# Forgetting attention rebuilt in a 16-head, 1024-token fp32 decoder step: split q and v stored by the projections, minima instead of maxima, GpSimd normalisation, halves copied by VectorE and added by DMA

## What is computed

```python
# layer 0: y = W_out(B * conv3(C * h)), then SwiGLU; layer 1: attention, then SwiGLU
k, v = split(x @ kv_w); logf = log_sigmoid(x @ f_w + f_b); cum = cumsum(logf)
q = x @ q_w
s = (q . k) * 64**-0.5 + cum[t] - cum[s]        # s <= t, else -inf
p = softmax(s); o = p @ v; y = o @ o_w
x = layer_norm(ALPHA * x + y)                    # after every mixer and every FFN
x = layer_norm(ALPHA * x + (silu(x @ g) * (x @ u)) @ w_down)
# outputs: y, k, v, logf, conv state, for the prompt and for the samples
```

## Time and profile before

| | |
|---|---|
| median of 3 runs | 2944.03 us (2940.56 to 2947.19) |
| span of the profiled execution | 2939.8 us |
| TensorE busy, mean granted clock | 2726.8 us, 0.951 |
| VectorE, ScalarE, GpSimd busy | 1279.7, 838.0, 822.3 us |
| k, v, q stage, us 1228 to 1545 | 317 us |
| between that stage and attention's first scores | 29 us |
| attention, us 1574 to 1981 | 407 us |

### The profile page before, as it was taken

The page is one execution under the profiler, slowest core; times in us unless marked ns, Lnnn a source line. Parts: engine busy times, 40 slices in busy tenths (PEclk is TensorE's granted clock), DMA queues, the critical chain, the costliest instruction groups (busy, mean ns, idle before and its releaser), DMA issues.

```text
span 2939.8 us, 44825 instructions
## 1 busy us (share of the span) xinstructions
PE 2726.8 (93%) x16971; PEld 2622.2 (89%) x16971; DVE 1279.7 (44%) x2212; ACT 838.0 (29%) x1463; POOL 822.3 (28%) x475
## 2 busy tenths in 40 slices
PE   8999959999999999699996889989799999999994
PEld 8999949999999999499994777779699999999994
DVE  3333582422222222850555888874733222222237
ACT  2111142111111111432224666652511111111114
POOL 2222252112212112532333333323612221212114
PEclk9999979999999999899997888889799999999996
DMA  4111101111111111022874454442011111111101
GB/s 131 43 50 43 45 22 44 44 44 44 46 56 44 51 44 44 15 74 77 262 245 129 125 133 124 123 126 65 22 44 44 44 57 45 51 44 44 51 15 58
DMA packets 214332, 206.47 MB, mean 70 GB/s; under 512 B 29239, under 2 KB 184887, under 8 KB 214188
## 3 DMA queue, kind: packets, MB, share of 16 engines
q1 hardware_dynamic: 209388, 187.25, 21.8%
q0 software_dynamic: 4800, 17.08, 1.7%
HBM read 178.76 MB, written 25.57 MB: 70 GB/s over the span
## 4 chain that ended last, share of the span: by engine, by line
PE 80%; DVE 10%; issue 5%; DMA 2%; ACT 1%; POOL 1%; SPq 0%; DVEq 0%; POOLq 0%; ACTq 0%
PE ps L1600 25%; PE ps L1601 24%; PE ps L1602 24%; DVE ss L1482 2%; PE ps L1859 2%; DVE ln_t L1271 1%; DVE ln_t L1275 1%; PE ps L1888 1%; DVE ln_d L1216 1%; DVE ptl L1507 1%; DMA k_prompt<-ktok 1%; PE ps L1874 1%; PE ps L1841 1%; PE ps L1837 1%; PE ps L1875 1%
## 5 line engine op out<-in xcount | busy, mean ns | idle before, releaser
L1600 PE MATMUL ps<-xh,whi 128*128 128x344 f32 x3288 | 1067.7, 325 | 28.2 <-POOL xl L663 18.0
L1601 PE MATMUL ps<-xl,whi 128*128 128x344 f32 x3288 | 1054.7, 321 | 0.0
L1602 PE MATMUL ps<-xh,wlo 128*128 128x344 f32 x3288 | 1054.5, 321 | 0.0
L617 POOL TENSOR_TENSOR wlo<-wraw,whi 128x1024 fp32r<-128x1024 f32 x197 | 481.3, 2448 | 1700.4 <-ACT whi L794 1700.4
L1600 PEld LDWEIGHTS ps<-xh,whi 128*128 128x128 f32 x3288 | 620.2, 189 | 56.8 <-POOL xl L663 34.3
L1602 PEld LDWEIGHTS ps<-xh,wlo 128*128 128x128 f32 x3288 | 621.8, 189 | 0.0
L1601 PEld LDWEIGHTS ps<-xl,whi 128*128 128x128 f32 x3288 | 621.6, 189 | 0.0
L1600 PE MATMUL ps<-zh,whi 128*128 128x344 f32 x1440 | 465.4, 323 | 17.4 <-DVE x L1343 9.4
L1601 PE MATMUL ps<-zl,whi 128*128 128x344 f32 x1440 | 463.7, 322 | 0.0
L1602 PE MATMUL ps<-zh,wlo 128*128 128x344 f32 x1440 | 461.7, 321 | 0.0
L1320 DVE TENSOR_TENSOR silu<-silu,ps 128x344 f32<-128x344 f32 x132 | 67.8, 513 | 875.6 <-PE ps L1602 875.6
(11 more groups left out here) (206 smaller groups left out, 2650.0 us busy)
## 6 DMA issues: line engine op xcount, KB each, us to landing
wraw<-ffn_w_gu SPq DMA_DIRECT2D x88, 512.0 KB, 3.8
wraw<-ffn_w_down SPq DMA_DIRECT2D x44, 512.0 KB, 3.5
kp<-cache_k SPq DMA_DIRECT2D x32, 512.0 KB, 5.4
vp<-cache_v SPq DMA_DIRECT2D x32, 512.0 KB, 3.5
wraw<-a_w_in SPq DMA_DIRECT2D x24, 512.0 KB, 3.8
wraw<-kv_w SPq DMA_DIRECT2D x16, 512.0 KB, 5.3
qd<-q_t SPq DMA_DIRECT2D x32, 256.0 KB, 4.7
kd<-k_t SPq DMA_DIRECT2D x32, 256.0 KB, 5.3
```

The lines of the kernel that those rows point to most:

```text
L617: pool.tensor_tensor(wlo[:, s, :], wraw[:, s, :], f32(whi[:, s, :]), ALU.subtract).then_inc(w_lo, 1)
L1600: pe.matmul(out, w_h, m_h, start=start, stop=False)
L1601: pe.matmul(out, w_h, m_l, start=False, stop=False)
L1602: return pe.matmul(out, w_l, m_h, start=False, stop=stop)
```

## The change

It rebuilds attention and what feeds it.

1. `q_t` in HBM gets two planes. `take_q` on ScalarE writes the high part, scaled with -QSCALE, and `q_low` on VectorE the low part, both out of PSUM; only `q_low` frees the bank. v goes the same way into a new `v_t` (`v_tokens`, `v_low`). In attention `qa` and `vhl` are loaded ready split; `qk_high`, `v_high`, attention's `q_low` and `v_low` go.
2. The scores are negated, the mask is +1e30, the bias row is `ccum`, VectorE takes the minimum, and ScalarE's exponential has scale -1. The negation L1488 goes.
3. Scores, mask, transposes and values leave out the blocks above the diagonal (`span`, `turned`).
4. All of `norm` runs on GpSimd as a tensor_scalar. GpSimd also does both halves of k's split (`k_split`).
5. VectorE copies all 128 rows of `values` to `oe` (`o_take`). SP stores the upper half to `o_t`, and GpSimd's queue adds the lower half there with an accumulating DMA (`add_halves`). The last pair is added in SBUF as before.
6. `wraw` and `wlo` share memory. A load of a weight block therefore waits until the unit that used the slot is over (`used`), instead of for the split of the block before.
7. `o_t` is read through five buffers, and the first unit of `o` takes k-block 7 of all chunks last (`first_o`).

```diff
+        whi = wa.put("whi", [P, WR, WCOLS], F32R)
+        wlo = wa.put("wlo", [P, WR, WCOLS], F32R)
+        wraw = Area(W_AT + WR * WCOLS * 4).put("wraw", [P, WR, WCOLS], F32)
...
+            def used(unit):
+                return full[NCH - 1], unit - WR + 1
...
             def load_kvq(it, keys):
+                first = isinstance(it, int) and it == 0
+                ends = ffn[0].at("down", FG * KB * NCH)
+                load(n0 + 3 * it, n0, w_kv[:, :, bass.ds(it * P + D, P)], ends if first else used(g0 + 3 * it))
...
+                    load(n0 + 3 * it + 1 + j, n0 + 1 + j, src, ends if first and j == 0 else used(g0 + 3 * it + 1 + j))
...
             for m in range(WR):
-                load(SLOTS["o"] + m, SLOTS["o"] + m, w_o[:, :, m * P:(m + 1) * P])
+                load(SLOTS["o"] + m, SLOTS["o"] + m, w_o[:, :, m * P:(m + 1) * P], used(UNITS["o"] + m))
             load_samples(KB - 1)
...
+            with sp.Fori(0, KB - 1) as b:
+                next_qk(b, 0)
+                load_v_page(b, 2)
+                load_v_page(b, 3)
+                next_qk(b, 1)
+                next_v(b, 0)
                 store_head(b, 0)
+                load_v_page(b + 1, 0)
+                load_v_page(b + 1, 1)
+                next_v(b, 1)
                 store_head(b, 1)
...
+            def k_split(b, e):
...
+                pool.wait_ge(qk_in[e], loaded)
+                pool.tensor_copy(kh[e][:, :], kd[e][:, :]).then_inc(at["khi"], 1)
                 pool.wait_ge(at["khi"], 2 * b + e + 1)
                 pool.tensor_tensor(kl[e][:, :], kd[e][:, :], f32(kh[e][:, :]), ALU.subtract).then_inc(at["klo"], 1)
...
+                for t in range(2):
+                    pool.tensor_scalar(ss[j][:, t, 0:span(st, t)], ss[j][:, t, 0:span(st, t)], ri[:, j, t:t + 1], None,
+                                       ALU.mult).then_inc(at["pnorm"], 1)
...
+                pool.dma_start(o_t[bass.ds(b, 1), e * DH:(e + 1) * DH, :].rearrange("a p t -> (a p) t"),
+                               oe[e][DH:P, :], accum_op=ALU.add).then_inc(oe_add[e], 16)
...
             with pool.Fori(0, KB - 1) as b:
+                norm(b, STEPS)
+                k_split(b + 1, 0)
+                for st in range(STEPS + 1, PAIR):
+                    norm(b, st)
+                add_halves(b, 0)
+                norm(b, PAIR)
+                k_split(b + 1, 1)
+                for st in range(PAIR + 1, PAIR + STEPS):
+                    norm(b, st)
+                add_halves(b, 1)
...
+                    act.activation(hl[:, 0, c * CH:c * CH + w], ps[:, c, 0:w], ACT.Copy, scale=-QSCALE).then_inc(kv["qh"], 1)
...
+            with dve.Fori(0, KB // 2) as it:
+                q_low(it, 0)
+                v_low(it)
+                q_low(it, 1)
...
             with dve.Fori(0, NS // 2) as it:
+                v_low(it + KB // 2)
                 for j in range(2):
...
-                    dve.wait_ge(at["sdr"], 2 * s + 2)
-                    dve.tensor_scalar(nm[:, j, :], mx[:, j, :], -1.0, None, ALU.mult).then_inc(at["neg"], 1)
...
+                dve.tensor_copy(oe[e][:, j * 2 * P:(j + 1) * 2 * P], ps[:, 6 + st % 2, 0:2 * P]).then_inc(at["odone"], 1)
...
+                    pe.wait_ge(at["pnorm"], 2 * s + 2)
...
+                blocks = [(2 * g, 0), (2 * g, 1)] + [(2 * g + 1, t) for t in range(2) if t or g < j]
...
+def span(st, t):
+    return P * (2 * (st % STEPS) + t + 1)
+def turned(st, g):
+    return P * (3 if g == st % STEPS else 4)
```

More of the change, by code:

```diff
@@ L231, in build @@
         ftok = fa.put("ftok", [P, TB + 1, H], F32)
+        assert fa.at <= SC_AT
         aa = Area(XH_AT)
[L234 to L239, removed]
@@ L269, in build @@
+        oraw = Area(XH_AT).put("oraw", [P, OS, TP], F32)
         ya = Area(XH_AT)
@@ L685, in _, with store_q, store_k @@
             low(n0 + 2, n0 + 2)
-            def store_block(x_t, x, j, ready):
+            def store_q(it, j):
+                g = g0 + 3 * it + 1 + j
+                split = pool.to_reg(g + 1)
+                apart(pool)
+                for c in range(NCH):
+                    pool.wait_ge(free[c], split)
+                pool.dma_start(q_t[bass.ds(2 * it + j, 1), :, :, :].rearrange("a s p t -> p (a s) t"), f32(hl[:, :, :])).then_inc(kv["qdma"], 16)
+            def store_k(it, j):
+                ready = pool.to_reg(2 * it + j + 1) if not isinstance(it, int) else 2 * it + j + 1
@@ L749, in head @@
-            def head(b, e, last=False):
-                for j in range(2):
-                    for t in range(2):
-                        norm(b, e, j, t)
-                if not last:
-                    k_low(b + e, 1 - e)
-                norm(b, e, 2, 0)
-                if not last:
-                    v_low(b + e, 1 - e)
-            k_low(0, 0)
-            v_low(0, 0)
-            with pool.Fori(0, KB - 1) as b:
-                head(b, 0)
-                head(b, 1)
-            head(KB - 1, 0)
@@ L768, in _ @@
+            for st in range(STEPS, PAIR):
+                norm(KB - 1, st)
             proj_low("o", 2)
@@ new lines, in take_k, with v_tokens @@
+            def take_k(it, j):
+                x = 2 * it + j - KB
+                if not (isinstance(it, int) and it == KB // 2):
+                    act.wait_ge(kv[f"x{j}dma"], 16 * (it - KB // 2))
+                act.wait_ge(kv["kt"], 2 * x + 2)
+                take(g0 + 3 * it + 1 + j, stage[1 + j], 1, x, 1.0, kv["x"])
+            def v_tokens(it):
+                if not (isinstance(it, int) and it == 0):
+                    act.wait_ge(kv["vdma"], 16 * it)
+                    act.wait_ge(kv["vtdma"], 16 * it)
+                for half in range(2):
+                    act.wait_ge(kv["vt"], 2 * it + 2 + half + 1)
+                    act.activation(vtok[:, 4 * half:4 * half + 4, :].rearrange("p a d -> p (a d)"),
+                                   ps[:, 3 + half, :], ACT.Copy).then_inc(kv["vtok"], 1)
+                    act.activation(vst[:, :, 4 * half:4 * half + 4, 0, :].rearrange("p e i d -> p i e d"),
+                                   ps[:, 3 + half, :].rearrange("p (i e d) -> p i e d", i=4, e=2), ACT.Copy).then_inc(kv["vh"], 1)
@@ L1084, in step @@
                         exps(b, st + 2, g)
-                if st % PAIR == 1:
-                    v_high(b + st // PAIR, 1)
-                if st == STEPS + 1 and not last:
-                    v_high(b + 1, 0)
-                if st >= 2:
-                    o_half(b, st - 2)
-            qk_high(0, 0)
-            v_high(0, 0)
+                if last and st >= 2:
+                    o_half(st - 2)
             for st in range(2):
@@ L1533, in step @@
                     inverse(b, st + 2)
-                    norm(b, st + 2)
-                if st >= 2:
-                    o_sum(b, st - 2)
+                if last and st >= 2:
+                    o_sum(st - 2)
+                elif st >= 2:
+                    o_take(b, st - 2)
             def sample_sum(b):
```

544 lines of the change are left out of this document (296 added, 248 removed).

## The result

The changed kernel takes 2965.83 us (median of 4 runs, 2960.05 to 2968.18), the kernel before 2944.66 beside it: a ratio of 1.0068, 95% interval 1.0054 to 1.0083. It is slower by about 0.7%, where 2934 and a gain were forecast. The profiled execution has a span of 2964.9 us, 25.1 over that of before.

What follows compares the result with a forecast made beforehand. TensorE (busy 2726.8 of 2939.8 us) was taken as the bound, with attention's waits running through VectorE. Attention's gains (-61, -3, +1.5) and costs elsewhere (+24, +11, +13, +3, +1) summed to -10.5: 2934 us, 8 in 10 within 2893 to 2983.

Steps and rivals of the forecast that it cites:

- attention, ramp, drain: Attention: a pair of heads falls from 49.6 to 42 us, 61 gained; its start gains 3, its drain loses 1.5.
- first q unit: Feeding stage: TensorE waits 23 us for its bank, freed by q_low behind the scalings of x; +24 (17 to 30).
- k iterations: Feeding stage: third weight slot's copy comes 4.5 us later, delaying ktok and v's bank; 3.7 x 3 = +11 (0 to 20).
- last pages: Before attention: last eight pages queue behind the third w_o load, so pst comes at 1588; +13 (8 to 20).
- layer norms, first `o`: Layer norms 0 and 2: copy delays a square and GpSimd's sums, +3; oraw's two late buffers, +1.
- GpSimd's price: Attention's norm on GpSimd: 1.2 ns a column, bounds 0.8 and 2.4; 5.5 us a head plus overheads.
- The rival: Attention: GpSimd's norms become the chain; at 2.4 ns a pair takes 48 us, 2982; chance 0.17, half way (2958) 0.15.
- The split of head 0: Attention: GpSimd, blocked on loads, ends next head 0's k split at 24 us; at 2.4 ns 25.1, norms late.
- falls to its floor: Attention: rival in which the clock stays up and a pair takes 39 to 40 us, 2913; chance 0.2.
- the 3.8 laid out: Attention: TensorE's remaining waits, for step 2's scores bank and pt_low at a head's start, 3.8 us a pair.
- the time at half clock: Attention: sample pages and stretches at half clock stay, costing TensorE 3 us a pair instead of 6.4.
- TensorE's work at full clock: Attention: a pair's 37.7 us at 2.4 GHz loses 2.6 by skipped blocks, transposes and mask, leaving 35.1.

Runs made afterwards that it cites:

- e1: Changed kernel with GpSimd copying ss in place instead of multiplying it by the reciprocal of the row sum: 2936.8 us, ratio to before 0.9974.
- e12: Changed kernel with the next head 0's q and k loads issued ahead of the page, v load and store: 2965.1 us, ratio to before 1.0068.
- e17: Changed kernel with feeding stage mended, q and k loads early, widest step's norm on VectorE and adding DMAs later: 2897.2 us, ratio to before 0.9840.
- e5: Changed kernel with the first q_low, v_low and q_low ahead of the 16 scalings of x on VectorE: 2948.8 us, ratio to before 1.0011.
- e6: Changed kernel with the first ktok copy and k_prompt store ahead of the third weight slot's copy and split: 2965.1 us, ratio to before 1.0068.
- e10: Changed kernel with q_low and ktok first, and SP's weight-slot and last page loads reordered, attention untouched: 2930.9 us, ratio to before 0.9954.
- e8: Changed kernel with the value halves copied out of PSUM by ScalarE instead of VectorE: 2961.7 us, ratio to before 1.0062.
- e14: Changed kernel with early q and k loads and the widest step's norm on VectorE, one step later behind pt_low: 2954.7 us, ratio to before 1.0029.
- e15: Changed kernel with early q and k loads, widest step's norm on VectorE, adding DMAs behind two more norms and a k split: 2935.3 us, ratio 0.9965.
- e16: Changed kernel with only the adding DMAs moved, behind two more norms and a k split in GpSimd's list: 2965.9 us, ratio to before 1.0068.
- e2: Changed kernel with all of the norm moved from GpSimd to VectorE, behind the reciprocal: 2980.8 us, ratio to before 1.0111.

## Why the prediction was wrong

It missed the span by 35.6 us (-10.5 against +25.1). By its own terms:

| term | forecast | measured |
|---|---|---|
| attention, ramp, drain | -62.5 | -35.0 |
| first q unit | +24 | +20.9 (25.2 - 4.3) |
| k iterations | +11 | +21.3 (46.5 - 25.2) |
| last pages | +13 | +14.3 (60.8 - 46.5) |
| layer norms, first `o` | +4 | +3.6 (25.1 + 35.0 - 20.9 - 21.3 - 14.3) |

These are TensorE's own shifts. ScalarE's weight copies would mislead: the second of the first k iteration starts 28.2 us later than before (1449.71 for 1421.49), while TensorE's unit there is 24.6 later. A load now waits for a unit's end, so its copy comes later, but here not so late that TensorE waits for it.

**The step that failed is GpSimd's price**, "I take 1.2, nearer the one-input rows". It is 2.5 ns a column, just above the dear bound of 2.4, and a head's norms take 14.3 us where I had 5.5 and overheads. The two-input subtraction in the earlier trace rows was the row that came near it; the cast and memset of the earlier trace rows were not. (Nor does the cheap bound of 0.8 follow from them: 207 ns for 128 columns are 1.6 a column.) I took the price of a copy, which is 5.9 us a head in e1. At that price, in e1, attention (first scores to first unit of `o`) takes 344.2 us and not 374.8: 65.6 gained on before, against a forecast of 62.5. That one term is worth 30.6 us, which is 27.5 of the miss and 3 more. By its ratio e1 is 0.3% faster than the kernel before, at 2936.8 beside a forecast of 2934. That this is so near is in part luck, since the k iterations cost 10 us more than I had and the pair was better than my 42.

The Trainium skill's GPSIMD Engine Reference (4.1 Engine selection) calls one-input work "roughly line-rate". The copy is near that, 1045 ns for 1024 columns, where VectorE's tensor_scalar takes 748; GpSimd's tensor_scalar, which also reads one tensor, isn't, at 2848 ns and 2769 with an immediate. Its two-input figure, by which the prediction had the pair at 48, would have given the right sign, but too long a pair.

**The rival was named and its mechanism right, its size wrong.** At 2.4 ns the pair was to take 48 us; at 2.5 it takes 44.3. The split of head 0, which was to decide, waits for its load in fact (16.1 us in 250), but issuing that load earlier (e12) gave nothing. Between the copy's 0.8 ns a column and 2.5 the pair moves by 3.8 us, where I had 6 between 1.2 and 2.4. That the adds' wait takes over once the norms are fewer was not in the prediction; GpSimd's wait for the store was in none of its steps.

**The pair without that.** With cheap norms I had 42: the rival "falls to its floor" at 39 to 40 was nearer. e1 has 40.5 and e17 39.9, at a granted clock of 0.96, so with some 8% of the time at 1.2 instead of 2.4 GHz, where before it was 26%. TensorE is busy 222.3 of 250 us in e17, so 4.4 us of a pair are still idle, near the 3.8 laid out; what I had too high is the time at half clock (3 us lost; 4% of 39.9 is 1.6) and TensorE's work at full clock (35.1 us; 35.5 busy less 1.6 is 33.9).

**First q unit**: right in place, 3 us too high in sum, and e5 shows the scalings as the cause. The wait was 17.3 and not 23 us. TensorE came to it 0.7 us later (1284.4, less the 4.3 from before, for 1279.33), and the last scaling ended at 1301.2, less 4.3 at 1296.9, where I had 1298 + 3.3. I had let the scalings take their time of before, 19.4 us; they took 15.1. Two of them had been slow there, each while GpSimd subtracted (VectorE, then GpSimd, in the kernel before):

```profile
1281.21 3.31 DVE L1404 SCALAR_TENSOR_TENSOR x<-xl,x 128x1032 f32<-128x1032 f32 x1
1292.67 3.48 DVE L1404 SCALAR_TENSOR_TENSOR x<-xl,x 128x1032 f32<-128x1032 f32 x1
...
1280.47 2.96 POOL L617 TENSOR_TENSOR wlo<-wraw,whi 128x1024 fp32r<-128x1024 f32 x1 [8.07 <-ACT whi L794]
1292.65 2.39 POOL L617 TENSOR_TENSOR wlo<-wraw,whi 128x1024 fp32r<-128x1024 f32 x1 [7.41 <-ACT whi L794]
```

In the changed kernel that subtraction fell elsewhere, and all eight took 1.23 us. Another 2.8 us are the half clock behind the wait (14.2 for 11.4), a little more than my 1 or 2.

**k iterations: the second step that failed.** "Of the 4.5 us only 0.8 (...) is covered: 3.7 x 3" was mis-sized. From the third unit of the first k iteration to that of the last, three iterations, TensorE takes 133.9 us (1446.11 to 1580.03) for 112.0 (1421.47 to 1533.48), 7.3 more for each. Of these 21.9 us, 15.0 are waits of TensorE (6.1, 4.9 and 4.6 us, ahead of each first k unit, less 0.6 before), and the rest is mostly the unit behind each (14.4 us for 12.2), which starts at half clock (0.65 us a matmul). The `ktok` chain is there, but e6 shows that it was only one of two. The other I saw for the last pages only: SP loads each iteration's first slot behind eight pages, and with the shared memory that load may not be issued before the unit that used the slot is over. I had taken the order of SP's list as harmless inside the loop, and the half clock behind each wait not at all. e10 mends both and has the iteration back at 37.3.

**Last pages**: right, 14.3 for 13, in part by luck. `pst` ended at 1634.7, which less the 46.5 from before is 1588.2, forecast 1588. But the sums ended 3 us sooner than I had (1621.2 less 46.5 is 1574.7, for 1578), and `pst` followed them by 13.5 us and not by 10. **FFNs**: unchanged, as said. From the last broadcast to the last down group FFN 0 takes 753.2 us before and 753.8 after, FFN 1 752.3 and 752.2. **Halves by VectorE**: I gave them no price; they take 408 ns each, and with ScalarE doing them (e8) the whole takes the same within 0.1%.

## What to carry to other kernels

What GpSimd took for a row of 1024 columns hung here on the operation (1045 ns for a copy, 2769 for a multiplication by a constant), not on how many tensors it read: where the trace has no row of it, use the dearest row of that engine until one measurement settles it. When an engine's list waits for a DMA in the middle of work that others wait for, relieving the engine may give little until the wait is moved too (e14, e15), and moving the wait may give nothing while the engine is full (e16): change both. When a buffer is shared to save memory, its loads have to wait longer and so does what stands behind them in the queue; the queue's list must be ordered anew with it (e10). And a stage's shift is to be read on the engine whose time is asked for, since another engine's can move without costing anything.

## What the runs showed of the hardware

- GpSimd: a copy of 128x1024 fp32 in place takes 1045 ns, the same with a multiplication 2848, with an immediate 2769, a subtraction of two tensors 2399. VectorE's multiplication took 748 ns for 1024 columns and 613 for 768 when GpSimd did no norms (e2):

```profile
L1597 DVE TENSOR_SCALAR ss<-ss,ri 128x1024 f32<-128x1024 f32 x11 | 8.2, 748 | 0.0
...
L1597 DVE TENSOR_SCALAR ss<-ss,ri 128x768 f32<-128x768 f32 x10 | 6.1, 613 | 0.0
```

- In the kernel before, with GpSimd normalising beside it, the same 768 columns took VectorE 1927 ns, three times as long. e2 shows the same in one trace: its norm of 384 columns on VectorE took 0.42 us in three of the eleven cases in us 1700 to 1950, and 0.9 to 2.5 us in the eight that began while GpSimd's two-input subtraction (L803) ran. The Trainium skill's SBUF — State Buffer ("SBUF: two separate sides") says that VectorE and GpSimd take turns on a shared pair of ports, one instruction blocking the other; these times agree with that. Not every slow case lasted as long as GpSimd's instruction plus VectorE's own time (1927 ns against 1470 + 613), and no run here tells why.
